# Channel sums of twelve norms: a matrix of ones as weights and the squares moving, with the root and reciprocal taken on all partitions

## The reference

```python
def rms_norm(x, g):
    xf = x.astype(jnp.float32)
    y = xf * lax.rsqrt(jnp.mean(xf * xf, axis=-1, keepdims=True) + EPS)
    return (y * g.astype(jnp.float32)).astype(x.dtype)

def _modulate(x, g, shift, scale):
    return _rmsnorm(x, g) * (1 + scale[:, None, :]) + shift[:, None, :]

for layer in range(DEPTH):                       # first block
    h = rms_norm(x, norm_mix[layer])
    ...
    x = x + mix.astype(x.dtype)
    x = x + conv_ffn(rms_norm(x, norm_ffn[layer]), ff_w_up[layer], ...)
    gate = jax.nn.sigmoid(rms_norm(x, norm_ple[layer]) @ ple_w_gate[layer])
    x = x + (gate * (p[layer] @ ple_w_proj[layer])).astype(x.dtype)
for i in range(DEPTH):                           # second block
    h = _modulate(x, norm_g[i, 0], mods[:, 0, 0], mods[:, 0, 1])
    x = x + MACARON_W * mods[:, 0, 2][:, None, :] * _swiglu(h, ffn_w_in[i, 0], ffn_w_out[i, 0])
    ...
return _rmsnorm(x, final_g)
```

## Time and profile before

| | |
|---|---|
| time, three runs | 4079.7, 4082.8, 4087.09 us; median 4082.8 us |
| profiled execution, its own time | 4082.99 us |
| its span (first to last instruction) | 4081.2 us, so 1.8 us lie around it |
| busy | PE 3983.8 us (98%), DVE 1995.2 (49%), POOL 1337.3 (33%), ACT 693.3 (17%) |
| granted PE clock, mean | 0.991 of full speed |
| DMA | 386.86 MB, mean 95 GB/s |

### The profile page before, as it was taken

How to read it: one execution, slowest core, us unless ns; L and a number is a source line. 1 busy time by engine, 2 the same in 40 slices (tenths; PEclk the granted TensorE clock), 3 DMA queues, 4 the chain that set the end, 5 groups by cost and what they waited for, 6 DMA issues and landing times. The chain is left out here.

```text
span 4081.2 us, 46434 instructions
## 1 busy us (share of the span) xinstructions
PE 3983.8 (98%) x18322; PEld 3065.2 (75%) x18322; DVE 1995.2 (49%) x3654; ACT 693.3 (17%) x1506; POOL 1337.3 (33%) x1138
## 2 busy tenths in 40 slices
PE   9999999998999999999999999999999989999999
PEld 4458888754588887888844588888888537858888
DVE  5537767448476763433245444324333744444333
ACT  2321110123211101200024310011001321211000
POOL 0004444203344341344403434444443042024443
PEclk9999999999999999999999999999999999999999
DMA  3115444210245342222210122222222232112222
GB/s 131 42 57 195 166 175 151 99 67 32 83 170 183 142 177 71 93 83 85 89 67 24 42 90 86 88 88 83 85 86 88 72 103 71 36 58 84 89 82 78
DMA packets 134215, 386.86 MB, mean 95 GB/s; under 512 B 38928, under 2 KB 47248, under 8 KB 124272
## 3 DMA queue, kind: packets, MB, share of 16 engines
q1 hardware_dynamic: 119216, 305.23, 22.7%
q10 hardware_dynamic: 13968, 75.70, 4.9%
q0 software_dynamic: 816, 2.97, 0.2%
HBM read 375.26 MB, written 8.39 MB: 94 GB/s over the span
## 5 line engine op out<-in xcount | busy, mean ns | idle before, releaser
L959 PE MATMUL bank<-normed,weight_ring 128*128 128x256 f32 (+1 forms) x3600 | 1012.0, 435 | 4.0 <-ACT normed L1873 1.6
L959 PEld LDWEIGHTS bank<-normed,weight_ring 128*128 128x128 f32 x3600 | 676.7, 189 | 294.4 <-issue 222.9
L959 PE MATMUL bank<-area_b,weight_ring 128*128 128x256 f32 (+3 forms) x2128 | 600.4, 430 | 5.1 <-issue 2.8
L959 PEld LDWEIGHTS bank<-area_b,weight_ring 128*128 128x128 f32 (+2 forms) x2128 | 396.9, 187 | 170.8 <-issue 126.3
L860 POOL TENSOR_TENSOR area_d<-weight_ring 128x512 f32<-128x512 f32 (+1 forms) x106 | 133.3, 1257 | 950.5 <-PE bank L959 857.9
L959 PE MATMUL bank<-area_b 128*128 128x256 f32 (+2 forms) x1656 | 364.5, 377 | 18.0 <-DVE area_b L3136 12.8
L959 PE MATMUL bank<-area_a,weight_ring 128*128 128x256 f32 (+2 forms) x1424 | 373.9, 416 | 2.2 <-DMA weight_ring<-in_weights_dram 2.0
L860 POOL TENSOR_TENSOR area_b<-weight_ring 128x512 f32<-128x512 f32 (+1 forms) x102 | 128.1, 1256 | 726.5 <-PE bank L959 638.6
L959 PE MATMUL bank<-area_b,area_d 128*128 128x256 f32 x1560 | 358.5, 382 | 6.0 <-issue 5.6
L959 PEld LDWEIGHTS bank<-area_b 128*128 128x128 f32 (+1 forms) x1656 | 299.5, 192 | 76.0 <-issue 15.2
L959 PEld LDWEIGHTS bank<-area_b,area_d 128*128 128x128 f32 x1560 | 297.0, 191 | 49.0 <-issue 6.3
(11 more groups left out here) (334 smaller groups left out, 4973.5 us busy)
## 6 DMA issues: line engine op xcount, KB each, us to landing
weight_ring<-in_weights_dram SPq DMA_DIRECT2D x429, 512.0 KB, 4.6
area_b<-in_weights_dram ACTq DMA_DIRECT2D x48, 1024.0 KB, 4.9
weight_ring<-in_weights_dram SPq DMA_DIRECT2D x27, 1024.0 KB, 4.8
area_b<-in_weights_dram ACTq DMA_DIRECT2D x48, 512.0 KB, 6.1
weight_ring<-in_weights_dram SPq DMA_DIRECT2D x43, 384.0 KB, 4.3
weight_ring<-in_weights_dram SPq DMA_DIRECT2D x29, 256.0 KB, 4.0
weight_ring<-in_weights_dram SPq DMA_DIRECT2D x38, 128.0 KB, 4.0
low_scratch<-area_d SPq DMA_DIRECT2D x16, 256.0 KB, 2.0
```

What stands on the lines that cost most here:

```text
L959: i = pe.matmul(out, lhsT, rhs, start=start, stop=stop)
```

## The change

Per half of norms 1 to 12:

- The six `pick` products become two: the constant `ones` (128x128) is the weights, and 256 columns move, first of `RB`, then of the last square. The other of the two last squares is added into `RB` beforehand by DVE (`add_half_square`, 128x256, both inputs in SBUF), at a place of its own in `add_last`, `add_out` and `ple`. The sums come out as 128x256 in PSUM, the same on all partitions.
- `half_root` takes the root of 128x256 and writes it into `RB`, `half_rstd` takes the reciprocal of 128x256 in place in `RB`.
- `half_spread` is gone with all its calls, and `half_scaled` reads `RB` (SBUF) where it read the bank (PSUM).
- On ACT, `half_square(n, 2)` moves from behind the first four shifts (`norm_tail`) to right behind `half_root(n, 0)`.

```diff
             def half_sum(n, half):
-                out = half_bank(n, half)[:, 0:2]
+                out, cols = half_bank(n, half), (half0, half1)[half]
                 if half == 0:
                     pe.wait_ge(small_done[3], at["s"] // 4)
...
-                for x in range(3):
-                    if x == 0:
-                        pe.wait_ge(S("squares_added"), 5 * (n + 1))
-                    else:
-                        pe.wait_ge(S("half_squares"), 4 * (n - 1) + 2 * half + x)
-                    for e in range(2):
...
-                        mm(out, source, const("pick", t, NB)[:, 2 * half:2 * half + 2], x == 0 and e == 0, last,
-                           S("norm_summed") if last else None)
-            def half_spread(n, half):
-                pe.wait_ge(S("rstd_ready"), of_norm(n) + half + 1)
-                for t in (2 * half, 2 * half + 1):
-                    mm(half_bank(n, half)[:, t * P:(t + 1) * P], RSTD[:, t:t + 1].to_broadcast([P, P]), const("ident"),
-                       True, True, S("rstd_spread") if t % 2 else None)
+                pe.wait_ge(S("half_added"), 2 * (n - 1) + half + 1)
+                mm(out, const("ones"), RB[:, cols], True, False)
+                pe.wait_ge(S("half_squares"), 4 * (n - 1) + 2 * half + 2)
+                k = last_halves(n)[2 * half + 1][0]
+                mm(out, const("ones"), SQ[:, x_order(n).index(k) % 2, cols], False, True, S("norm_summed"))
...
             def half_root(n, half):
                 act.wait_ge(S("norm_summed"), of_norm(n) + half + 1)
-                a(ROOT[:, 2 * half:2 * half + 2], half_bank(n, half)[:, 0:2], ACT.Sqrt, scale=1 / 1024, bias=vec("eps", 0))\
-                    .then_inc(S("norm_root"), 1)
+                cols = (half0, half1)[half]
+                a(RB[:, cols], half_bank(n, half), ACT.Sqrt, scale=1 / 1024, bias=vec("eps", 0)).then_inc(S("norm_root"), 1)
...
             def norm_tail(n):
                 shifted(n, 0, 0, 4)
-                half_square(n, 2)
                 half_square(n, 3)
...
                 half_root(n, 0)
+                half_square(n, 2)
                 norm_tail(n)
...
             def half_rstd(n, half):
                 dve.wait_ge(S("norm_root"), of_norm(n) + half + 1)
-                dve.reciprocal(RSTD[:, 2 * half:2 * half + 2], ROOT[:, 2 * half:2 * half + 2]).then_inc(S("rstd_ready"), 1)
+                cols = (half0, half1)[half]
+                dve.reciprocal(RB[:, cols], RB[:, cols]).then_inc(S("rstd_ready"), 1)
...
-                dve.wait_ge(S("rstd_spread"), of_norm(n) + half + 1)
+                dve.wait_ge(S("rstd_ready"), of_norm(n) + half + 1)
                 for k in norm_order(n, half)[first:last]:
-                    stt(H[:, k, cols], X[:, k, cols], gain(n, k), half_bank(n, half)[:, cols], ALU.mult, ALU.mult)\
+                    stt(H[:, k, cols], X[:, k, cols], gain(n, k), RB[:, cols], ALU.mult, ALU.mult)\
                         .then_inc(out, 1)
...
+            def add_half_square(n, half):
+                k = last_halves(n)[2 * half][0]
+                cols, slot = (half0, half1)[half], x_order(n).index(k) % 2
+                dve.wait_ge(S("half_squares"), 4 * (n - 1) + 2 * half + 1)
+                dve.wait_ge(S("squares_added"), 5 * (n + 1))
+                tt(RB[:, cols], RB[:, cols], SQ[:, slot, cols], ALU.add).then_inc(S("half_added"), 1)
...
                 for which, (k, half) in enumerate(last_halves(n)):
                     if which == 3:
                         norm_begun(n)
+                        add_half_square(n, 1)
                     add(m0 + 6 + which, k, (half0, half1)[half])
                     if which == 0:
                         add_square(n, 5)
+                    if which == 1:
+                        add_half_square(n, 0)
                 norm_ended(n)
```

More of the change, by code:

```diff
@@ L475, in half_bank @@
         def half_bank(n, half):
-            return bank[7 if half == 0 else 6 if n in (3, 7, 10) else 2]
+            return bank[7 if half == 0 else 6 if n in (3, 7, 10) else 2][:, half1 if half else half0]
         ROOT, RSTD = SM[:, 88:92], SM[:, 92:96]
@@ L1100, in project_out @@
                     for k in range(DB):
-                        if half and k == 4:
-                            half_sum(n, 0) if j == 6 else half_spread(n, 0)
+                        if half and j == 6 and k == 4:
+                            half_sum(n, 0)
                         mm(pbank(m)[:, cols], kept(w0 + DB * (j - 6) + k), rhs(k)[:, cols], k == 0, k == DB - 1,
@@ L1214, in up @@
                         half_sum(n, 1)
-                    if (p, what) == (1, "P1"):
-                        half_spread(n, 1)
                     if n in CONVOLVED and what == (PARTS[-1] if p else "P4"):
@@ L1254, in down @@
                         part_is_free(what, *((name, q - 1) if q else (f"up{n}", ff - 1)))
-                    if q == LAST and not conv and what == "P3" and c == 0:
-                        half_spread(n + 1, 0)
                     sums = conv_down_sum if conv else lambda j, i: down_sums(ff, j)[:, i, :]
@@ L1272, in ple @@
                 w0 = at["w"]
-                project_in(n, lambda k: H[:, k, :], lambda j, k: half_spread(n, 1) if (j, k) == (1, 0) else None, 10)
+                project_in(n, lambda k: H[:, k, :], lambda j, k: None, 10)
                 for j in range(2, 6):
@@ L1287, in ple @@
                         for k in range(kb):
-                            if rhs is H and half and k == (6 if j == 6 else 4):
-                                half_sum(n + 1, 0) if j == 6 else half_spread(n + 1, 0)
+                            if rhs is H and half and j == 6 and k == 6:
+                                half_sum(n + 1, 0)
                             mm(pbank(m)[:, cols], kept(w0 + 10 * j + first + k), rhs[:, k, cols], k == 0, k == kb - 1,
@@ L1618, in _ @@
                         half_sum(10, 1)
-                    if half == 0 and k == 3:
-                        half_spread(10, 1)
             at["w"] = w0 + RW_PARTS["k"][0] + 4 * DB
@@ L1863, in _ @@
             half_sum(12, 1)
-            half_spread(12, 1)
             begin("end")
@@ L2038, in ple @@
                 half_root(n + 1, 0)
+                half_square(n + 1, 2)
                 ready_for(ACT.Sigmoid)
@@ L2567, in up_gelu, with add_last @@
                 last.then_inc(sem, 1)
-            def add_last(name, t, sub, between, rooted, begun):
+            def add_last(name, n, t, sub, between, rooted, begun):
                 p1, u2, u3, u4 = (copy_of(what, LAST) for what in ("p1", "u2", "u3", "u4"))
@@ L2665, in add_conv @@
                     else:
-                        add_last(f"down{n}", 3 * q + 2, None, squares, lambda: None, lambda: None)
+                        add_last(f"down{n}", n + 1, 3 * q + 2, None, squares, lambda: None, lambda: None)
             def ple(n, between={}):
@@ L2688, in ple @@
                         norm_begun(n + 1)
+                        add_half_square(n + 1, 1)
                     done(dve, m)
@@ L2697, in ple @@
                         add_square(n + 1, 5)
+                        add_half_square(n + 1, 0)
                 norm_ended(n + 1)
@@ L2996, in begun @@
                     also()
-                add_last(name, t, sub, squares, lambda: half_rstd(n, 0), begun)
+                add_last(name, n, t, sub, squares, lambda: half_rstd(n, 0), begun)
             up_silu(6)
```

8 lines of the change are left out of this document (removed).

## The result

| | us |
|---|---|
| before, median of 20 runs | 4084.4 (4079.7 to 4090.7) |
| after, median of 20 runs | 4090.6 (4083.5 to 4095.1) |
| ratio | 1.0016, 95% interval 1.0010 to 1.0022 |
| forecast | 4085.6, range 4069 to 4093, "no change" |

The kernel is slower by 0.16%, inside the 0.2% that the forecast called no change, and inside its range. The interval doesn't reach 1.0, so the loss is real, and it goes the way that the forecast's sum had it. The time is 5.0 us above the forecast: 1.6 of that is before itself, whose median of 20 runs is 4084.4 where the forecast started from 4082.8, and 3.4 is the change, which costs 6.2 us between the medians for the 2.8 forecast. The profiled execution took 4094.9 us, its span is 4093.0.

A forecast was written before the change was run, and what follows sets the result against it. The prediction took PE, busy 98% of the span, as the bound, with DVE's chain as late in front of the feed-forwards. Gains of 8.2 us and losses of 10.9, net 2.8 slower with rounding, gave 4085.6 us, range 4069 to 4093.

The forecast's parts named there:

- the forecast's sum: All norms together: 8.2 us gained, 10.9 lost, net 2.8 us slower with rounding.
- The bound and PE's savings: PE, busy 98%, sets the end; fewer products spare it 0.845 us per half, 1.69 per norm, 20.3 us if nothing waits.
- Root and reciprocal: Chain from sum to scaling: root from 0.26 to about 0.46 us, reciprocal from 0.17 to about 1.75, hidden where DVE waited.
- The scaling: Scalings on DVE, now with two SBUF inputs, take turns with POOL: about 1.0 us more for each that meets it.
- The first rival: Scalings in the feed-forward norms don't feel POOL: 13.2 us faster, 4069.6 us, -0.32%; chance 0.16.
- the second (full exclusion, a pitch of 1.67): DVE's scalings and POOL exclude each other altogether: 0.26 us more on 27 instructions, 4092.6 us, +0.24%; chance 0.15.
- Which scalings meet POOL: Slow scalings in norms 1, 4, 6, 9 and 11, some 22 of 192; half additions or additions to `X` also meet POOL.
- from DVE's lateness to PE's loss: Late scalings delay PE's token-sum products: loss 4.9 us in norms 1 and 4 together, 2.6 in 9, 2.3 in 6, 1.1 in 11.

The follow-up runs named there:

- experiment 1: After, with the root written back to the PSUM bank, reciprocal in place there and scalings reading it from there: 4071.8 us, ratio 0.9974 to before.
- experiment 2: Before plus a copy of the spread 128x256 into RB per half: first kernel, scalings reading RB, 4099.8 us (1.0044); control, reading the bank, 4086.2 (1.0007).
- Experiment 3: GpSimd's weight sums cut to 2 columns for two tiles behind norm 9: first kernel, on after, 4083.4 us (1.0006); control, on before, 4083.9 (1.0002).
- experiment 5: Second half's root moved ahead of the first half's last two shifts: first on after with the operand in the bank, 4072.7 us (0.9977); second on after, 4090.6 (1.0018).
- Experiment 4: After, with constant products keeping PE busy ahead of its wait for the first token sum in the feed-forward norms: 4087.5 us, ratio 1.0008 to before.

## Why the prediction held, and where its sum was off

**The bound and PE's savings: right.** The pair of products costs 0.86 us as forecast, and norms 2, 5, 7 and 10, with nothing in the way, give 1.8 to 1.85 us each for the 1.69 taken. The busy time falls by 6.7 us and not by 20: in the same row stand 6.4 us of the low clock (1.7 + 3.0 + 1.7) and 3.8 us more busy time for the same 715 instructions ahead of norm 1; some 3.4 us isn't placed. A busy PE isn't a PE at full speed.

**Root and reciprocal: right**, 0.46 and 1.753 us. Their place, where DVE waited before, hides them: in experiment 1, with both in place, each feed-forward norm comes earlier.

**The scaling: right in mechanism and size.** The forecast had the turns at 1.0 us each; those well inside POOL's bursts lie 1.41 us apart and take 1.48 to 1.49, the others 0.40 and 0.48. Experiments 1 to 3 show the condition from three sides: operand back to the bank, operand moved alone, POOL's work away. The first rival (no effect of POOL) falls with L2419's maximum, the second (full exclusion, a pitch of 1.67) with the 1.41. The Trainium skill's rule in "SBUF — State Buffer", section "Who interferes with whom", held in kind: one SBUF input, no contention (0.47 us beside the burst), two, contention. Taken to the letter, as full blocking, it would have given 4092.6 us; the runs show turns.

**Which scalings meet POOL: nearly right.** 25 slow scalings for the forecast's some 22. In norms 1 and 4 seven instructions are slow, as forecast, but all are scalings; the half addition, which was to be the first of the seven, takes 0.42 us. Norm 6 has three and the addition to `X` (1.52 us), for four and the addition. Norm 9 has six and the half addition, seven for six instructions, 1.0 us more.

**The step that failed is the one from DVE's lateness to PE's loss.** The forecast let PE lose exactly the time it waits and then go on at full speed. Where no low clock follows, its losses are near what is measured: 2.5 us against 2.26 in norms 1 and 4 (norm 1 of experiments 3 and 5, norm 4 of after less its 3.0), 2.3 against 2.65 in norm 6, 1.1 against 1.1 in norm 11, and in norm 9 2.6 and the 1.0 of the seventh instruction against 3.9. What it lacks is the low clock behind the wait: 1.7 us in norm 1, 3.0 in norm 4 and 1.7 in norm 9 of the profiled execution, 6.4 together, for waits of about 2 us. Experiment 4 speaks for the wait as what brings it, in one profiled execution. With the 6.4 and the 1.0 the forecast's 2.8 becomes 10.2, and the table's column has 10.3. The medians lie only 6.2 us apart. Part of the difference is the stretch around 630 us, where this execution falls the shorter way; how often the low clock comes in the runs that aren't profiled stays open, so that the 3.4 us by which the medians exceed the forecast can't be divided further. That the forecast came within this much of the time is in part luck: a missing term of up to 6.4 us was still inside its range.

**The first rival priced the better version.** It gave 4069.6 us for scalings that don't feel POOL. Experiment 1 makes them so by leaving the operand in the bank and measures 4071.8, 0.26% under before and 0.42% under after; its column of the table sums to -12.7 us and its median lies 12.1 under before's, the rival's sum was -13.2. The forecast didn't think of the bank as the way there.

## What to carry to other kernels

Before moving an operand of a VectorE instruction from PSUM to SBUF, look at what GpSimd does in the same stretch: here the 0.40 us from one scaling to the next became up to 1.41 at 25 of 192, and this outweighed the 20 us of TensorE work that the forecast counted as saved. When you follow a late engine to TensorE, price its wait with the low clock that can follow it. An idle gap ahead of an instruction, as the one ahead of the second reciprocal, tells what releases it and not what would be next: with two shifts moved aside, the root waited for TensorE's sums, and of the gap of 0.9 to 1.0 us 0.57 stayed in two norms and all of it in a third.

## What the runs showed of the hardware

- Behind a wait of 2.0 to 2.1 us TensorE had the lower clock for 3.0 to 5.6 us in norms 1, 4 and 9 of after and in norms 4, 9 and 11 of experiment 5's variant of after, and not in norms 6 and 11 of the one and 1 and 6 of the other, whose waits are as long (1.99 to 2.11): six of ten. Experiment 3's kernel (norms 4 and 6, not 1 and 11) and the first of experiment 2 (norm 4, not 1) make it nine of 16. What decides between them isn't settled. With a wait of 0.27 it stayed at 1.00.
- A wait of TensorE costs more than the profile shows as idle time. The next start, 0.22 us away without it, comes 0.38 us and the idle time after the last one, and the start behind that after 0.29 to 0.32 us: 1.4 us over the waits of norm 9.
- GpSimd pays for the turns too, and unequally: beside slow scalings L860 and L863 mostly take 1.44 to 1.54 us for 1.27 to 1.28 in experiment 1; L862 and L865, at 1.27 to 1.33, hardly more than there. In norms 1 and 4 it pays first: L860 takes 1.76 us there, and the half addition that starts 0.21 us behind it in norm 1 takes its fast 0.42.
- A VectorE instruction with one operand in the bank, right behind a half addition of 1.48 us, takes its 0.47 beside the same GpSimd burst, and the scalings behind it, with two in SBUF, take 1.09 and then 1.48 again: the contention is by instruction, not by stretch.
